# The last block's softmax normalisation of each attention step, taken from VectorE to ScalarE

## The reference, cut to what matters

```python
s = einsum('bhqd,bhkd->bhqk', qb, k) * scale      # fox adds cum[q] - cum[k]
s = where(key_pos <= qpos, s, -inf)
p = softmax(s, axis=-1)
o = einsum('bhqk,bhkd->bhqd', p, v)
```

## Time and profile before

| | |
|---|---|
| time, median of 3 runs | 1788.53 us (1787.32 to 1789.47) |
| the profiled execution | 1785.2 us, its span 1783.5 us |
| TensorE busy | 1719.1 us, 96% of the span |
| VectorE, ScalarE, GpSimd busy | 952.3 us (53%), 787.3 us (44%), 412.4 us (23%) |
| granted TensorE clock | 0.994 over the span, 1.00 from 62 to 521 us |

### The profile page before, as it was taken

One profiled execution on the slowest core, in us unless ns is written; L12 is line 12 of the kernel. 1 busy time (PEld: TensorE's weight loads), 2 busy tenths in 40 slices (PEclk: granted clock), 3 DMA queues, 4 the chain that ended last, 5 costly groups with the idle time before them and its releaser, 6 DMA issues.

```text
span 1783.5 us, 25326 instructions
## 1 busy us (share of the span) xinstructions
PE 1719.1 (96%) x8460; PEld 1427.8 (80%) x8460; DVE 952.3 (53%) x1736; ACT 787.3 (44%) x1373; POOL 412.4 (23%) x555
## 2 busy tenths in 40 slices
PE   7899998999989999899999999999999999999998
PEld 6777877898978888578878888888888788888886
DVE  6677775776773334675455555433346555555332
ACT  6667766566662224333333333322363433333222
POOL 3546565555530001300211111011003211111000
PEclk9999999999999999899999999999999999999999
DMA  4112122333323334123333333333332233333332
GB/s 135 51 44 62 38 61 60 85 74 70 82 62 99 98 94 138 52 78 106 95 94 95 94 94 94 114 97 98 94 94 71 83 98 96 98 96 92 92 97 86
DMA packets 284312, 154.39 MB, mean 87 GB/s; under 512 B 12655, under 2 KB 278770, under 8 KB 284242
## 3 DMA queue, kind: packets, MB, share of 16 engines
q1 hardware_dynamic: 281858, 148.95, 29.1%
q0 software_dynamic: 2336, 4.47, 1.1%
q10 hardware_dynamic: 48, 0.07, 0.0%
HBM read 147.02 MB, written 2.16 MB: 84 GB/s over the span
## 4 chain that ended last, share of the span: by engine, by line
PE 82%; DVE 6%; ACT 4%; POOL 4%; issue 3%; DMA 0%; ACTq 0%; DVEq 0%; POOLq 0%
PE ps L361 67%; PE ps L970 5%; PE ps L2382 2%; POOL w_split L318 1%; PE ps L802 1%; PE ps L823 1%; PE ps L784 1%; ACT w_split L304 1%; POOL w_split L320 1%; DVE tmp L1298 1%; PE ps L673 1%; PE ps L836 1%; POOL arena_r L1455 1%; DVE arena_r L1334 1%; PE ps L810 1%
## 5 line engine op out<-in xcount | busy, mean ns | idle before, releaser
L361 PE MATMUL ps<-u,w_split 128*128 128x512 f32 x3825 | 911.0, 395 | 13.2 <-DVE u L1962 8.4
L361 PEld LDWEIGHTS ps<-u,w_split 128*128 128x128 f32 x3825 | 714.9, 189 | 176.8 <-DVE u L1962 8.7
L320 DVE TENSOR_TENSOR w_split<-w_raw,w_split 128x1024 fp32r<-128x1024 f32 (+1 forms) x221 | 268.2, 1213 | 434.2 <-ACT w_split L304 434.1
L304 ACT CAST w_split<-w_raw 128x1024 fp32r<-128x1024 f32 (+4 forms) x321 | 289.1, 915 | 416.1 <-PE ps L361 381.2
L361 PE MATMUL ps<-arena_r,w_split 128*128 128x512 f32 x1824 | 417.2, 390 | 1.7 <-DVE arena_r L2522 1.7
L361 PEld LDWEIGHTS ps<-arena_r,w_split 128*128 128x128 f32 x1824 | 341.9, 188 | 74.1 <-DVE arena_r L2522 3.3
L2302 POOL TENSOR_TENSOR tmp<-tmp 128x512 f32<-128x512 f32 x44 | 56.9, 1293 | 423.7 <-ACT tmp L2287 423.7
L318 POOL TENSOR_TENSOR w_split<-w_raw,w_split 128x256 fp32r<-128x256 f32 x168 | 122.2, 757 | 16.1 <-ACT w_split L304 15.4
L1811 POOL TENSOR_TENSOR tmp<-tmp 128x512 f32<-128x512 f32 x40 | 56.6, 1415 | 269.8 <-ACT tmp L1770 234.5
L970 PE MATMUL ps<-u,w_split 128*128 128x264 f32 x768 | 105.8, 287 | 2.4 <-POOL w_split L318 2.2
L970 PEld LDWEIGHTS ps<-u,w_split 128*128 128x128 f32 x768 | 98.6, 189 | 5.0 <-POOL w_split L318 2.7
(11 more groups left out here) (265 smaller groups left out, 1588.2 us busy)
## 6 DMA issues: line engine op xcount, KB each, us to landing
w_raw<-in_w_in_dram SPq DMA_DIRECT2D x118, 256.0 KB, 3.2
w_raw<-in_w_ffn_gate_dram SPq DMA_DIRECT2D x88, 256.0 KB, 3.1
w_raw<-in_w_ffn_up_dram SPq DMA_DIRECT2D x88, 256.0 KB, 3.1
w_raw<-in_w_ffn_down_dram SPq DMA_DIRECT2D x64, 256.0 KB, 3.0
w_raw<-in_w_in_even_dram SPq DMA_DIRECT2D x32, 256.0 KB, 3.1
w_raw<-in_w_in_odd_dram SPq DMA_DIRECT2D x32, 256.0 KB, 3.1
w_raw<-in_w_ffn_down_dram SPq DMA_DIRECT2D x32, 192.0 KB, 2.6
w_raw<-in_w_br_mla_dram SPq DMA_DIRECT2D x16, 256.0 KB, 3.0
```

Source lines behind the costliest of these rows:

```text
L304: ins = act.copy(dst, src)
L320: ins = eng.tensor_tensor(lo, r, hi, ALU.subtract)
L361: last = pe.matmul(out_ap, w_tile(c, ws, k - n0), moving(k, ms), start=start and n == 0, stop=stop and n == len(total) - 1, skip_group_che ...
```

## The change

For block 7 of each step, VectorE makes only the reciprocal. The product with it is an activation of ScalarE, a scaled copy in place, placed directly behind the block's exponential and ahead of act_p(6). It waits for the reciprocal (`recip`) and gives the same signal (`normed`) that VectorE gave. Blocks 0 to 6 are as before. No transfer is added or moved.

```diff
--- before.py
+++ after.py
@@ -1204,6 +1204,8 @@
                 if b == 0 and joined:
                     act_low(act, s - 2, 1)
                 act_exp(act, pr, b)
+                if b == 7:
+                    act_norm_last(act, pr)
                 if b == 1 and gemm != "mla":
                     act_low(act, s - 2, 0)
                 if attn == "fox" and b == 0:
@@ -1294,8 +1296,15 @@
             dve.wait_ge(sem("exped"), 8 * pr + b + 1)
             dve.reciprocal(ri[:, b:b + 1], rs[:, b:b + 1]).then_inc(sem("recip"), 1)
             dve.wait_ge(sem("recip"), 8 * pr + b + 1)
+            if b == 7:
+                return
             p = prob[:, b % 2, 0:META + n_real(b)]
             dve.tensor_scalar(p, p, ri[:, b:b + 1], None, ALU.mult).then_inc(sem("normed"), 1)
+
+        def act_norm_last(act, pr):
+            act.wait_ge(sem("recip"), 8 * pr + 8)
+            p = prob[:, 1, 0:META + n_real(7)]
+            act.activation(p, p, ACT.Copy, scale=ri[:, 7:8]).then_inc(sem("normed"), 1)
 
         def dve_p(dve, pr, b):
             dve.wait_ge(sem("p_hi"), 8 * pr + b + 1)
```

## The result

| | before | changed |
|---|---|---|
| time, median | 1789.36 us (6 runs, 1787.32 to 1793.22) | 1795.83 us (6 runs, 1795.02 to 1797.48) |
| span of the profiled execution | 1783.5 us | 1793.7 us |
| VectorE busy, ScalarE busy | 952.3, 787.3 us | 940.9, 798.7 us |

The ratio is 1.0036, with a 95% interval from 1.0025 to 1.0047: 6.4 us slower (4.5 to 8.4). The forecast was 4.8 us slower.

A forecast was written before the change was run, and what follows sets the result against it. TensorE was taken to bound the kernel (82% of the chain), so only its waits before each step's last transposes count. Step delays less gains in steps 8 and 9 sum to 4.82 us slower: 1793.3 us, range 1789.4 to 1796.5.

The forecast's parts named there:

- 1, 10 to 15: Seven steps where TensorE already waits: dve_p(6) 0.59 us late, nothing behind with slack over 0.07; 4.13 us in all.
- What was side by side becomes a row: At block 7, act_p(6) ran beside reciprocal and normalisation; now reciprocal, scaled copy, act_p(6) and dve_p(6) follow each other.
- The price of the copy: ScalarE's 128x528 scaled copy was taken as 0.70 us; bounds: 0.62 us gives +3.5 us, no overlap +6.4.
- The signs named ahead: Right if steps 10 to 15 show a 0.70 us copy and 1.15 us TensorE wait; wrong if copy under 0.62 or over 0.72.
- S + 1.12: Forecast start of dve_p(6), 1.12 us after S, the time at which VectorE began the normalisation before.
- Steps 2, 4 and 6: dve_p(6) 0.38 us late, slack at the second head's values takes up 0.11; 0.27 each, 0.81 us in all.
- Steps 3, 5 and 7: dve_p(6) 0.64 us late, TensorE busy with a projection gives 0.29 of slack; 0.35 each, 1.05 us in all.
- Steps 8 and 9: VectorE's normalisation, held up by GpSimd, took 1.93 and 2.10 us; moving it gains 0.83 and 1.02 us.
- Rival 1: Slack ahead of the second head's values partly absorbs the delay: 0 to +3.5 us, or -1.9; chance 0.21.
- Rival 2: Faster: timed runs hold more VectorE hold-ups behind GpSimd; six such steps give -4.2 us, 1784.3; chance 0.07.
- Rival 3: Shifted phases put another VectorE normalisation behind GpSimd's weights, 1.5 us each; two make +7.8, 1796.3 us; chance 0.10.
- Rival 4: The scaled copy brings a table load in each step, 20.5 us more, 1813.8 us; chance 0.02.

The follow-up runs named there:

- e1: The changed kernel with the scaled copy placed behind act_p(6) instead of ahead of it; median 1784.28 us, ratio to before 0.9976.
- e2: The changed kernel with the scaled copy on only the first 144 columns of block 7, 384 left unnormalised; median 1788.92 us, ratio to before 1.0001.
- e3: The kernel before with the change made in steps 8 and 9 alone; median 1787.03 us, ratio 0.9987.
- e4: The kernel before with GpSimd's low part of the next weights moved, in steps 8 and 9, behind its block 7 meta copy; 1786.58 us, ratio 0.9986.
- e5: The kernel before with the change made in steps 10 to 15 alone; median 1792.9 us, ratio 1.003.
- e6: The kernel before with two (step 8) and four (step 9) one-element VectorE memsets between last reciprocal and normalisation; one time, 1791.6 us.

## Why the prediction was right, point by point

Time and sign were right, the mechanism too; several sizes were off, and the loss of 6.4 us (6.0 by the sum below) is larger than the 4.8 forecast. The time, 1795.83 us, lies inside the range of 1789.4 to 1796.5, but 0.3 us above the forecast's own 1791.2 to 1795.5; 0.8 us of the distance to 1793.3 comes from the kernel before, whose median was 1789.36 and not 1788.53. Below, each step's delay is measured as in step 11, from its last reciprocal to its L829 matmuls.

| steps | forecast | measured, each | sum forecast | sum measured |
|---|---|---|---|---|
| 1, 10 to 15 | +0.59 | +0.66 to +0.69 | 4.13 | 4.74 |
| 2, 4, 6 | +0.27 | +0.44 to +0.47 | 0.81 | 1.37 |
| 3, 5, 7 | +0.35 | +0.45, +0.46, -0.03 | 1.05 | 0.88 |
| 16 | +0.68 | +0.76 | 0.68 | 0.76 |
| 8 | -0.83 | -0.77 | -0.83 | -0.77 |
| 9 | -1.02 | -0.94 | -1.02 | -0.94 |
| all | | | 4.82 | 6.04 |

- What was side by side becomes a row: right, and shown by e1 against the changed kernel (0.27 and 1.24 us of wait with the same copy) and by e2.
- The signs named ahead: act_p(6) 0.99 us later in step 11 for the forecast 0.95, TensorE's wait 1.24 for 1.15 there and 1.24 for 1.1 in step 9, 0.75 shorter for 0.8 in step 8, the stretch longer by 5.95 for 4 to 6. No normalisation of VectorE newly took over 1.5 us.
- The price of the copy: 0.70 forecast, 0.737 measured. I had named a copy over 0.72 us as a sign of error, and it is one, but of 0.04 us in a price and not in the mechanism:

```profile
...
L1307 ACT ACTIVATE tmp<-tmp,stats x16: 736/737/739, 87.9 to 521.5; 128x528 f32<-128x528 f32 x16
...
```

 The Trainium skill's formula (ScalarE: Activation LUTs, What ACT_TABLE_LOAD costs) gave an estimated 0.72, nearer than the rows' 0.70; the measured value is above both. For its overlap of 93 ns the trace has 381.32 + 0.74 - 381.96 = 0.10 us.
- The handoffs: S + 1.12 was forecast for dve_p(6), and it came at S + 1.20 (382.52 - 381.32). Half of the 0.08 is the copy; the rest is the way from act_p(6) to dve_p(6), where the 0.04 that I had taken was 0.10 and act_p(6) was 0.02 shorter. This term stands in all 16 steps, 1.3 us, and it is the main part of what was missing.
- Steps 2, 4 and 6: the slack of 0.11 us at the second head's values wasn't there. In step 4 the values begin 0.06 us behind dve_p(7) now instead of 0.18, but their eight matmuls then take until 179.69, 1.33 us against 1.22 before:

```profile
...
177.70 0.62 PE L829 MATMUL ps<-arena_r 96*64 96x512 f32 x2
...
```

 A modelled start that stands a little late is no slack by itself.
- Steps 3, 5 and 7: the slack of 0.2 to 0.3 us was real, and with S + 1.20 the forecast would have been 0.43. Step 7 had more of it, which I had passed over by taking it for one of their kind. There TensorE, with its last transposes done, waited for GpSimd's meta copy, which stood behind 3.01 us of weights. Before, then changed:

```profile
...
257.20 3.01 POOL L318 TENSOR_TENSOR w_split<-w_raw,w_split 128x256 fp32r<-128x256 f32 x4
...
259.04 0.60 PE L802 MATMUL ps<-cst,tmp 128*128 128x128 f32 x4
...
260.17 0.28 POOL L1500 TENSOR_TENSOR tmp<-tmp,ones 128x48 f32<-128x48 f32 x1
...
260.50 0.64 PE L810 MATMUL ps<-cst,tmp 128*96 128x128 f32 x4 [0.70 <-POOL tmp L1500]
...
```

```profile
...
260.17 2.81 POOL L318 TENSOR_TENSOR w_split<-w_raw,w_split 128x256 fp32r<-128x256 f32 x4
...
262.46 0.63 PE L802 MATMUL ps<-cst,tmp 128*128 128x128 f32 x4 [0.31 <-DVE arena_r L1312]
...
262.94 0.28 POOL L1509 TENSOR_TENSOR tmp<-tmp,ones 128x48 f32<-128x48 f32 x1
...
263.27 0.64 PE L810 MATMUL ps<-cst,tmp 128*96 128x128 f32 x4
...
```

 The step's last reciprocal is at 257.40 before and 260.35 changed. Counted from it, the transposes come 0.47 us later (2.11 against 1.64), and this fits into the wait of 0.70 us ahead of L810, which is gone. The meta copy itself comes 0.18 us sooner (2.59 against 2.77), now that VectorE's product is gone from beside the weights. This is the first rival, absorption, in one step of 16.
- Between the last matmuls of step 1 and the last reciprocal of step 2, 0.3 us came back, which I had not foreseen: TensorE's wait ahead of its transposes of block 2 shrank. What shortened it wasn't followed. Before, then changed:

```profile
...
103.89 0.52 PE L802 MATMUL ps<-cst,tmp 128*128 128x128 f32 x3 [0.78 <-DVE arena_r L1303]
...
```

```profile
...
104.53 0.52 PE L802 MATMUL ps<-cst,tmp 128*128 128x128 f32 x3 [0.49 <-DVE arena_r L1312]
...
```

 6.04 - 0.3 and 0.2 us of small shifts between the other steps make the 5.95.
- Steps 8 and 9: right within 0.08 us, shown by e3; the cause, GpSimd, by e4. One reading was off: step 9's normalisation didn't end with GpSimd's four instructions, at 323.73, but 0.30 us behind them, at 324.03. The sum doesn't use it.
- Rival 1, absorption: beyond the slack in the sum only in steps 2 and 7, 0.8 us. Rival 2, more hold-ups in the timed runs: not in a second profile. Rival 3, a hold-up that moves: not seen in either profile of the changed kernel; e5 shows that one can be missing from an untouched step, so the risk was real in kind. Rival 4, table loads: none at the copy, still six at the exponentials.
- Behind the attention nothing changed that stands out from the spread between two profiles of one kernel.

## What to carry to other kernels

Before an instruction is moved to an emptier engine, look at what is queued behind its new place. Here the copy was 0.24 us longer, but the cost was 0.7 us a step where GpSimd had not slowed VectorE, because act_p(6) had been running beside the product and now stood behind the copy. Behind act_p(6) in the same queue the same copy made the kernel 4.3 us faster than it was (3.2 of the stretch's 5.5 us came from the two steps in which VectorE had been held up).

A wait placed in the middle of an engine's list costs its own time and the length of what it guards, for everything queued behind it that was ready. And a product on VectorE that runs beside GpSimd's work may take four times its length; here moving the product gave part of this back (e3, 1.6 us) and moving GpSimd's work all of it (e4, 3.0).

## What the runs showed of the hardware beyond this

- A drop of TensorE's granted clock to 1.2 GHz for 3.4 us came at the same place, step 9, in both profiles of the changed kernel, in one of two of the kernel before, and in e4 and e6. It cost 1.1 us, more than most terms of the sum. A single pair of profiles would have charged it to the change.
- VectorE's 128x528 product, started during the second of GpSimd's four weight instructions, took 0.49 to 0.57 us or 1.9 to 2.1 us, and in e5's one profiled execution step 8 went from the long to the short with its own code and moment of start unchanged. When the product got in, GpSimd's group was longer by 0.2 us (3.02 against 2.79). What decides was not settled.
- ScalarE's copy showed no such spread: 736 to 739 ns in 16 steps, in 15 of them with GpSimd at its weights.
